# Four raw weight buffers in the second mixer of a two-block transformer kernel, with the loads written out

## The reference, cut to what matters

```python
h = rms_norm_2(x, norm1_g) * (1 + sc1) + sh1
proj = h @ w_in                                   # 1024 x 1792
q, k, v, cb, cc, ch, su, sv = jnp.split(proj, split_pts, axis=-1)
y_attn = sliding_window_attention(rms(q), rms(k), v, attn_sink, rel_bias)
y_conv = short_conv_mixer(cb, cc, ch, conv_w)
y_sgu = chunked_spatial_gating(su, sv, sgu_w, sgu_b)
merged = concat(rms(y_attn), rms(y_conv), rms(y_sgu))
x = x + g1 * (merged @ w_out)
h2 = rms_norm_2(x, norm2_g) * (1 + sc2) + sh2
x = x + g2 * peer_ffn(h2, ...)
```

## Time and profile before

| | us |
|---|---|
| median of 3 runs (lowest, highest) | 3368.8 (3363.11, 3371.12) |
| the profiled execution, device time | 3370.04 |
| its span in the profile | 3368.3 |
| TensorE busy in it | 2971.8 (88%) |
| mixer of layer 0, of layer 1 (stretch of the span) | 1240 to 1415, 2306 to 2481 |

### The profile page before, as it was taken

One profiled execution on the slowest core, in us unless ns is written; L12 is line 12 of the kernel. 1 busy time (PEld: TensorE's weight loads), 2 busy tenths in 40 slices (PEclk: granted clock), 3 DMA queues, 4 the chain that ended last, 5 costly groups with the idle time before them and its releaser, 6 DMA issues. The chain is left out here.

```text
span 3368.3 us, 46522 instructions
## 1 busy us (share of the span) xinstructions
PE 2971.8 (88%) x17972; PEld 2635.4 (78%) x17972; DVE 2346.4 (70%) x4119; ACT 1478.5 (44%) x2250; POOL 440.4 (13%) x249
## 2 busy tenths in 40 slices
PE   6899989598899767699889999996779988999998
PEld 5687777587777656599879978884669978998887
DVE  4868996487799746399597666675549688555665
ACT  3344333234433333254664445443334466445544
POOL 0100000010000000189400000000038910000000
PEclk9999999799999887799999999997789999999999
DMA  5424454443455343155316767774235513555654
GB/s 204 151 108 193 191 192 160 161 150 122 165 193 196 151 175 125 64 164 188 119 45 232 242 221 242 254 241 157 75 121 176 188 64 95 187 181 191 204 193 156
DMA packets 128286, 558.91 MB, mean 166 GB/s; under 512 B 15115, under 2 KB 18988, under 8 KB 102572
## 3 DMA queue, kind: packets, MB, share of 16 engines
q1 hardware_dynamic: 127052, 551.14, 47.3%
q10 hardware_dynamic: 1008, 4.72, 0.4%
HBM read 547.37 MB, written 9.49 MB: 165 GB/s over the span
## 5 line engine op out<-in xcount | busy, mean ns | idle before, releaser
L1843 PE MATMUL e_ps<-k_hhi,e_hi 128*128 128x256 f32 x2304 | 650.5, 282 | 29.0 <-POOL e_lo L1828 29.0
L1843 PE MATMUL e_ps<-k_hlo,e_hi 128*128 128x256 f32 x2304 | 647.0, 281 | 0.0
L1843 PE MATMUL e_ps<-k_hhi,e_lo 128*128 128x256 f32 x2304 | 645.6, 280 | 0.0
L2101 DVE TENSOR_TENSOR e_lo<-e_raw,e_hi 128x1024 fp32r<-128x1024 f32 x394 | 482.9, 1226 | 182.6 <-ACT e_hi L1925 178.4
L1925 ACT ACTIVATE e_hi<-e_raw 128x1024 fp32r<-128x1024 f32 x544 | 570.7, 1049 | 26.0 <-DMA e_raw<-down 24.9
L726 DVE TENSOR_TENSOR f_wlo<-f_raw,f_whi 128x2048 fp32r<-128x2048 f32 x156 | 356.5, 2290 | 183.3 <-ACT f_whi L559 183.1
L1843 PEld LDWEIGHTS e_ps<-k_hhi,e_hi 128*128 128x128 f32 x2304 | 436.2, 189 | 29.8 <-POOL e_lo L1828 29.6
L559 ACT ACTIVATE f_whi<-f_raw 128x2048 fp32r<-128x2048 f32 x156 | 296.7, 1912 | 341.0 <-DMA f_raw<-ws 280.9
L1843 PEld LDWEIGHTS e_ps<-k_hlo,e_hi 128*128 128x128 f32 x2304 | 435.6, 189 | 0.0
L1843 PEld LDWEIGHTS e_ps<-k_hhi,e_lo 128*128 128x128 f32 x2304 | 434.1, 188 | 0.0
L1828 POOL TENSOR_TENSOR e_lo<-e_raw,e_hi 128x1024 fp32r<-128x1024 f32 x150 | 385.4, 2585 | 88.5 <-ACT e_hi L1925 87.7
(11 more groups left out here) (333 smaller groups left out, 5225.9 us busy)
## 6 DMA issues: line engine op xcount, KB each, us to landing
f_raw<-ws SPq DMA_DIRECT2D x156, 1024.0 KB, 5.5
e_raw<-down SPq DMA_DIRECT2D x288, 512.0 KB, 3.4
e_raw<-up SPq DMA_DIRECT2D x256, 512.0 KB, 3.4
f_x<-ada SPq DMA_DIRECT2D x48, 512.0 KB, 3.6
s_raw<-ws SPq DMA_DIRECT2D x24, 1024.0 KB, 4.8
e_ada<-ada SPq DMA_DIRECT2D x48, 512.0 KB, 4.7
f_x<-out SPq DMA_DIRECT2D x4, 1024.0 KB, 6.0
f_const<-consts SPq DMA_DIRECT2D x2, 1104.0 KB, 7.1
```

Source lines behind the costliest of these rows:

```text
L1843: last = nc.tensor.matmul(psD(n), w, h, start=kt == 0 and i == 0, stop=kt == KT - 1 and i == 2)
L2101: V.tensor_tensor(lo[:, i % RING, :], raw[:, i % RING, :], hi[:, i % RING, :].bitcast(F32), ALU.subtract).then_inc(S["lo_dve"], 1)
```

## The change

`NRAW` in `second_mixer` goes from 2 to 4, with a semaphore for each buffer, and the loop over the later loads is written out, each waiting for the low part four units back:

```diff
-    NRAW, NW = 2, 3
+    NRAW, NW = 4, 3
...
-        raw_in = [S["raw0"], S["raw1"]]
+        raw_in = [S["raw0"], S["raw1"], S["raw2"], S["raw3"]]
...
-                with sp.Fori(1, U2 // NRAW) as i:
-                    for k in range(NRAW):
-                        sp.wait_ge(S["lo_ready"], i * NRAW + (k + 1 - NRAW))
-                        load(i * NRAW + k, k)
+                for u in range(NRAW, U2):
+                    sp.wait_ge(S["lo_ready"], u + 1 - NRAW)
+                    load(u, u % NRAW)
```

More of the change, by code:

```diff
@@ L1173, in second_mixer @@
         psS = cx.enter_context(nc.psum_tensor("s_psS" + str(l), [P, 4, CH], F32))
-        names = """in_x in_par in_bias raw0 raw1 hi_ready lo_ready unit_done acc_read small_ready small_read
+        names = """in_x in_par in_bias raw0 raw1 raw2 raw3 hi_ready lo_ready unit_done acc_read small_ready small_read
             dve_step pool_step const_ready in_mod mod_here x_sq x_rstd x_norm h_hi_ready h_lo_ready a_sq a_ss a_rstd a_qn
```

## The result

| | before | with the change |
|---|---|---|
| median, us (20 runs each) | 3370.91 | 3382.73 |
| lowest to highest | 3363.11 to 3379.76 | 3374.65 to 3389.5 |
| ratio to before, 95% interval | | 1.0030 [1.0020, 1.0039] |

The kernel became slower by 0.30%, or 10.1 us (6.7 to 13.1) by the ratio. The medians are 11.8 us apart. The forecast was +11.2 us. The profiled execution took 3376.14 us, where 3381.2 had been forecast for it.

What follows compares the result with a forecast made beforehand. The mixer's start was taken as bound by the landing of `s_bias` and 10.3 us of DVE work; four added loads at 2.8 us gave +11.2 us, other terms nothing, so 3380.0 us against a median of 3368.8, range 3372 to 3388.

Steps and rivals of the forecast that it cites:

- What bounds the kernel: Mixer start: `s_bias` lands, DVE works 10.3 us without a gap, TensorE starts q; TensorE never waits for weights after that.
- Two more loads ahead of the tables: SP's queue at each mixer's start: two added loads delay `s_bias` by 2.8 us each, +11.2 us over two mixers.
- SP issues two more ahead: SP's queue: `s_bias` is issued 0.96 us later, hidden by 7.3 us of backlog, so it costs nothing.
- DVE's idle time and TensorE's wait: Mixer start: DVE idles 11.7 us in place of 6.13, PE waits about 19 us in place of 13.5.
- Loads issued earlier: Units 2 to 11 in the mixer: ACT's waits for raw units go; gain 0 us, at most a few tenths.
- TensorE's clock: Start of q: the same slow clock, only later; bounded at 1 us per mixer either way, 2 us in all.
- No change: SP's queue: added loads cost `s_bias` little or nothing; 3368.8 us, up to 3375; chance 0.13.
- faster: TensorE's weight waits are hidden by the releasers, so prefetch gains; 3344 us at the very most; chance 0.04.
- Much slower: Each added load costs `s_bias` 4.8 us, or q's later start costs more slow clock; 3388 us; chance 0.08.
- three signs of being wrong: Mixer: `s_bias` lands after 12 to 13 us, landing order differs from issue, or q to cb over 1 us shorter.

Runs made afterwards that it cites:

- tables_between: The change, but with the two tables issued behind the second weight load and loads three and four behind them; ratio to the kernel before 1.0000.
- after_again: The change, unaltered, profiled and timed a second time; ratio to the kernel before 1.0021.
- mask_late_four: The change with four raw buffers, but VectorE's wait for the tables and the masking moved behind `h_rests`; ratio to the kernel before 0.9974.
- mask_late_two: Two raw buffers, loop of loads written out, VectorE's wait for the tables and the masking moved behind `h_rests`; ratio to the kernel before 0.9969.
- tables_first: The change, but with both tables issued ahead of all four weight loads; ratio to the kernel before 0.9996.
- unrolled_two: The change with NRAW at 2 and two semaphores, so only the written-out loop remains; ratio to the kernel before 1.0002.
- six: The change with NRAW at 6, so six weight loads ahead of the tables; ratio to the kernel before 1.0051.

## Why the prediction was right

*What bounds the kernel.* Right. q's start was bound by `s_bias` and the 10.3 us of DVE work behind it, to the tenth in both kernels. TensorE was not waiting for weights: from the first weight matmul to L1591 (L1590 now), the first DVE operation behind cb, it is 46.5 and 47.5 us before and 46.5 and 47.3 with the change. The last wait is still for TensorE:

```profile
1321.17 0.69 DVE L1590 TENSOR_TENSOR s_cy<-s_psA,s_cy 128x512 f32<-128x512 f32 x1 [0.40 <-PE s_psA L1264]
```

It is 0.40 us in place of 0.17, and was 0.40 us in layer 1 before. What an earlier ScalarE gains DVE, a few tenths at most, ends there.

*Two more loads ahead of the tables.* The mechanism is shown: taking only the tables' place back (tables_between) takes the whole loss back, and the dose of two, three, four and six loads gives an even rise. The term was sized at 2.8 us per load and measured 2.5 for the third and fourth, 2.75 for the next two. For four loads that is 10.0 us in place of 11.2. The timings give 10.1 and 7.1 us; the forecast of 11.2 is inside the interval of the first (6.7 to 13.1) and just outside that of the second (3.7 to 10.5). That the first two medians lie 11.8 us apart, so near the forecast, is in part luck: the second pair lies 7.9 apart.

The rate behind it: in the changed kernel the queue moved 425 GB/s for nine microseconds on end, from 5.0 to 14.0 us after the issue of x, where the kernel before had 351 from 3.0 to 12.0 us and 358 from 5.0 to 14.0. The figure of 358 GB/s that the Trainium skill gives as the limit of HBM for a core ("DMA: Bandwidth & Descriptors", Specifications) is not a limit in the stretch of the changed kernel, in which one core runs alone.

```profile
1249.05:1258.05 9.00, 1.95 (x9) 1.98 (x10) 2.48 (x9) 3.92 (x5) 0.89 (x2) 0.50 0.98 351
```

```profile
1251.05:1260.05 9.00, 3.65 (x16) 3.28 (x16) 2.48 (x9) 4.84 (x6) 0.89 (x2) 0.50 0.99 358
```

```profile
1249.19:1258.19 9.00, 3.65 (x16) 3.28 (x16) 2.48 (x9) 7.12 (x9) 0.90 (x2) 0.50 1.04 425
1258.19:1263.19 5.00, 0.00 (x0) 0.00 (x0) 0.00 (x0) 4.40 (x7) 0.00 (x0) 0.84 1.02 360
```

The first two are stretches of the kernel before, the other two are of the changed kernel (5.0 to 14.0 and 14.0 to 19.0 us after the issue of x), all with GB/s in the last column.

*SP issues two more ahead.* Right that it costs nothing, but I left it out of one of the marks. `s_bias` is issued 0.85 us later after x than before, so by the 5.0 us of b - a its time to landing grows by only 5.0 - 0.85 = 4.2 us. I gave 17 to 18 us in place of 12.1; 14.5 was measured, another 1.7 us less because the loads ahead of it landed that much earlier (mark a). In layer 1 it was 14.1 in place of 11.5.

*DVE's idle time and TensorE's wait.* 11.7 and 19 us were forecast, 9.4 and 16.8 measured in the first profile and 10.6 and 18.0 in layer 0 of after_again. There mark a is as in layer 0 of before (10.5 and 10.4 us), and the missing 1.1 us are the price of two loads, sized too high (b - a grew by 4.4 us, not 5.6); in the first profile mark a, which the prediction took as fixed, takes away 1.7 us more. One profile of each kernel was too little to read a shift of 3 us from: their marks c differ by 6.7 us in the two layers together, and by 7.5 us between the means of four mixers on two buffers (26.8) and four on four (30.5).

*Loads issued earlier.* Right: ACT's waits for raw units went, no gain came that shows. tables_between against the kernel before, and mask_late_four against mask_late_two, show it twice. The rule of the Trainium skill to issue the DMA early and wait for it late (same page, Rules for kernel authors) holds only for the transfer that is awaited; here the early issue of one was a late landing of another.

*TensorE's clock.* The same slow start, later, as expected: in the changed kernel the first weight matmul takes 0.80 us, as in the earlier trace rows, and the granted clock from 1274.60 to 1277.00 is 0.50. In between, the clock of that mixer had been at the upper level: it is 0.96 from 1258.00 to 1260.00 and 0.89 in the two microseconds behind, right after the transposes, while TensorE did nothing, and 0.50 again from 1262.00 on (that is the 0.84 in the last of the four rows above). In the same place before, and in layer 0 of after_again, it stayed at 0.50. It was gone before q could use it. The bound of 1 us per mixer was too tight, but at another place, below.

*The rivals.* No change and faster are out by the interval of both timings. Much slower, 4.8 us per load, is out by b - a. None of the three signs of being wrong came: `s_bias` took 14.5 us, the loads landed in the order of issue, and the stretch from q's start to the end of cb kept its length.

## What to carry to other kernels

Before you deepen a prefetch, look at what is issued behind it on the same queue. A loop that primes the buffers grows with their number, and a small table behind it may be what the first engine on the path waits for. And before looking for a better place in the queue, ask whether the wait has to stand where it is: moving one wait and one short operation behind work that doesn't need them won 9 to 10 us here, while four buffers in place of two won nothing that could be measured.

## What was not expected

*The start of a mixer comes in two forms.* Unit 0 is converted 8.5 to 8.9 us or 10.3 to 10.6 us after the issue of x (without tables_first, where more stands ahead of it), even within one execution. The late form goes with a lower rate of the queue. From 3.0 to 12.0 us after the issue of x the eight late mixers moved 347 to 398 GB/s and the ten early ones 391 to 410, but the size differs widely: in unrolled_two unit 0 was as late as before, at 379 to 384 GB/s in place of 351 and 359. In mask_late_four and six SP also issued `s_bias` a microsecond later in layer 0 than in layer 1. The cause stays open; no run aimed at it.

*The clock at the start of out.* Behind `mix` TensorE begins out at either level. Before, in layer 0, the granted clock of its first three microseconds is 1.00 and the second matmul took 0.39 us; with the change, at the same place, it is 0.50 and 0.63 us, behind the same transposes and the same 1.89 us without work:

```profile
1375.00 0.47 PE L1281 MATMUL s_psA<-s_whi,s_ahi 128*128 128x512 f32 x1 [1.89 <-issue]
1375.30 0.39 PE L1281 MATMUL s_psA<-s_wlo,s_ahi 128*128 128x512 f32 x1
```

```profile
1376.41 0.77 PE L1280 MATMUL s_psA<-s_whi,s_ahi 128*128 128x512 f32 x1 [1.89 <-issue]
1376.98 0.63 PE L1280 MATMUL s_psA<-s_wlo,s_ahi 128*128 128x512 f32 x1
```

From the end of `s_alo` to the store of x that is 25.0 us at the upper level and 26.3 to 27.7 otherwise. Over all profiles of this study both occur with two buffers and with four, so it isn't the change's. It is 2.2 of the 5.4 us by which layer 0's mixer is longer in the first profile of the changed kernel, and would have been taken for a part of the cost without the others. In layer 1 it went the other way, 26.3 us before and 24.9 with the change. What decides the level isn't known; no run aimed at it.
